# Idle products on TensorE at stage borders and in the mixers' fronts, and tiles turned by ordinary products

## The reference

```
# first block
z = rmsnorm(x) @ w_in ;  u, v, q, k, vv, gate, mq = split(z)
a = gelu(u) * (tril(w_s) @ rmsnorm(gelu(v)) + b_s)              # gMLP, 6 groups
b = softmax(q k^T/8 + cumsum(log_sigmoid(gate)) bias, causal) vv  # 6 heads
c = softmax(mq km^T/8) vm   with km, vm = rmsnorm(mem) @ w_mem_kv # 4 heads, 256 memory rows
x = x + rmsnorm([a, b, c] @ w_out)                              # M1
x = x + rmsnorm(relu(rmsnorm(x) @ w_ff1)^2 @ w_ff2)             # F0, width 4096
# second block, twice:  swiglu(h) = (silu(h @ wg) * (h @ wu)) @ wd, width 2816
x = x + swiglu(rmsnorm(x)) / 2                                  # F1, F3
x = x + sliding_window_attention(rmsnorm(x))                    # MA: 16 heads, 2 kv heads, window 128, sinks, T5 bias
x = x + latent_attention(rmsnorm(x))                            # MB: c = h @ w_in; q = norm(c_q) @ w_uq; k, v = norm(c_kv) @ w_ukv;
                                                                #     16 heads of 64 + 32 rotary, causal
x = x + swiglu(rmsnorm(x)) / 2                                  # F2, F4
```

## Time and profile before

| | us |
|---|---|
| runs | 1295.24, 1296.60, 1297.97 |
| median | 1296.6 |
| profiled execution | 1299.77 |
| its span | 1298.0 |
| PE busy | 1236.5 |
| DVE busy | 886.6 |
| ACT busy | 611.1 |
| POOL busy | 158.7 |

### The profile page before, as it was taken

How to read it: one execution, slowest core, us unless ns; L and a number is a source line. 1 busy time by engine, 2 the same in 40 slices (tenths; PEclk the granted TensorE clock), 3 DMA queues, 4 the chain that set the end, 5 groups by cost and what they waited for, 6 DMA issues and landing times.

```text
span 1298.0 us, 17912 instructions
## 1 busy us (share of the span) xinstructions
PE 1236.5 (95%) x7062; PEld 1065.0 (82%) x7062; DVE 886.6 (68%) x1078; ACT 611.1 (47%) x786; POOL 158.7 (12%) x164
## 2 busy tenths in 40 slices
PE   7998899999899999979999999999999869999998
PEld 7995799999788888866888888888888757888887
DVE  4886565565676776675866776866776475866675
ACT  5556534344443444576543444444344485544342
POOL 2431212012210000240100000100001340100000
PEclk9998899999999999999999999999999889999999
DMA  9773268695685556452555565655553313555530
GB/s 295 223 214 98 67 168 207 163 246 165 172 283 181 191 194 193 145 167 77 190 183 181 191 194 162 201 190 182 182 179 121 122 33 99 194 184 182 185 129 33
DMA packets 165401, 219.62 MB, mean 169 GB/s; under 512 B 13676, under 2 KB 143792, under 8 KB 165212
## 3 DMA queue, kind: packets, MB, share of 16 engines
q1 hardware_dynamic: 155356, 212.28, 51.8%
q0 software_dynamic: 9984, 6.49, 2.9%
HBM read 213.26 MB, written 5.25 MB: 168 GB/s over the span
## 4 chain that ended last, share of the span: by engine, by line
PE 85%; DVE 8%; ACT 4%; issue 1%; POOL 1%; DMA 0%; SPq 0%; DVEq 0%; ACTq 0%
PE ps L276 26%; PE ps L251 14%; PE ps L253 14%; PE ps L252 14%; PE ps L278 13%; DVE w_lo L232 2%; PE ps L555 1%; POOL scratch L799 1%; ACT w_hi L225 1%; PE ps L580 1%; PE ps L568 1%; ACT h_both L436 1%; DVE h_both L444 1%; DVE arena L658 1%; DVE scratch L806 0%
## 5 line engine op out<-in xcount | busy, mean ns | idle before, releaser
L225 ACT CAST w_hi<-raw 128x2048 fp32r<-128x2048 f32 x197 | 374.1, 1899 | 431.5 <-PE ps L278 274.3
L232 DVE TENSOR_TENSOR w_lo<-raw,w_hi 128x2048 fp32r<-128x2048 f32 x194 | 443.1, 2285 | 170.5 <-ACT w_hi L225 169.7
L276 PE MATMUL ps<-h_both,w_hi 128*128 128x512 f32 x1408 | 500.0, 399 | 4.6 <-DVE h_both L444 4.6
L278 PE MATMUL ps<-h_both,w_lo 128*128 128x256 f32 x1408 | 395.2, 281 | 0.0
L276 PEld LDWEIGHTS ps<-h_both,w_hi 128*128 128x128 f32 x1408 | 265.2, 188 | 70.6 <-issue 5.5
L278 PEld LDWEIGHTS ps<-h_both,w_lo 128*128 128x128 f32 x1408 | 266.5, 189 | 1.4
L251 PE MATMUL ps<-w_hi,act_hi 128*128 128x512 f32 x480 | 188.3, 392 | 1.4 <-DVE act_lo L1047 1.4
L253 PE MATMUL ps<-w_hi,act_lo 128*128 128x512 f32 x480 | 187.4, 390 | 0.0
L252 PE MATMUL ps<-w_lo,act_hi 128*128 128x512 f32 x480 | 187.2, 390 | 0.0
L283 DVE TENSOR_REDUCE arena<-ps 128x512 f32<-128x1024 f32 x88 | 107.8, 1225 | 82.4 <-PE ps L278 82.1
L251 PE MATMUL ps<-w_hi,h_both 128*128 128x256 f32 (+3 forms) x324 | 110.6, 341 | 10.2 <-DVE h_both L444 5.0
(11 more groups left out here) (237 smaller groups left out, 1300.9 us busy)
## 6 DMA issues: line engine op xcount, KB each, us to landing
raw<-in_ffn_wg SPq DMA_DIRECT2D x44, 1024.0 KB, 5.4
raw<-in_ffn_wu SPq DMA_DIRECT2D x44, 1024.0 KB, 5.4
raw<-in_ffn_wd SPq DMA_DIRECT2D x44, 1024.0 KB, 4.9
raw<-in_w_ff SPq DMA_DIRECT2D x32, 1024.0 KB, 17.2
raw<-in_w_in SPq DMA_DIRECT2D x8, 1024.0 KB, 11.8
raw<-in_a_w_in SPq DMA_DIRECT2D x5, 1024.0 KB, 5.4
raw<-in_w_out SPq DMA_DIRECT2D x4, 1024.0 KB, 5.1
raw<-in_a_w_out SPq DMA_DIRECT2D x4, 1024.0 KB, 5.0
```

Source lines behind the costliest of these rows:

```text
L225: nc.scalar.copy(w_hi[:, b % RING, 0:n], raw[:, b % RAW, 0:n]).then_inc(hi_ready, 1)
L232: nc.vector.tensor_tensor(w_lo[:, b % RING, 0:n], raw[:, b % RAW, 0:n], w_hi[:, b % RING, 0:n].bitcast(F32), ALU.subtract).then_inc(lo_rea ...
L276: nc.tensor.matmul(ps[:, bank + f, :], hi[:, k, f * P:(f + 1) * P], h_both[:, k, :, :].rearrange("p a b -> p (a b)"), start=k == 0, stop=F ...
L278: last = nc.tensor.matmul(ps[:, bank + f, 0:TOK], lo[:, k, f * P:(f + 1) * P], h_both[:, k, 0, :], start=False, stop=k == KD - 1, skip_gro ...
```

## The change

Three edits. **Turned tiles:** `turned()` issues `nc.tensor.matmul(to, source, ident)` where `nc.tensor.transpose(to, source, ident)` stood, at L391, L568, L967, L968, L1890, L1913, L1987 and L2040; 344 tiles in all. The transposes of the norms' gains (L1862) and of the gMLP's biases (L1891) stay. **Idle products:** `keep_busy(bank, n)` issues n products of `ident` with 256 columns of `tri` into a PSUM bank that nothing reads then. **Places:** 4 before the gains' landing, 5 behind the turn of mem, 5 behind the second projection, 4 before M1's wait for v, in M1's attention 4, 2, 2 ahead of rounds 2, 3, 4; at the border to F0 5 ahead of the turns, 2 amid them and 2 behind, to F1 2, 3, 2, at the other five 0, 0, 3; in MA's attention 1 and 3 ahead of rounds 2 and 3; in MB 6 and 3 behind the latent turns, 6 before q and k are first turned, and 6, 2, 3, 3 ahead of rounds 0 to 3. They are 90 together.

```diff
+        def turned(to, source):
+            return nc.tensor.matmul(to, source, ident[:, :], start=True, stop=True, skip_group_check=True)
+        def keep_busy(bank, count):
+            for _ in range(count):
+                nc.tensor.matmul(ps[:, bank, 0:TOK], ident[:, :], tri[:, 0:TOK], start=True, stop=True, skip_group_check=True)
         def product(to, still, moving, start, stop):
...
+        TURN_IDLE = {2: (5, 2, 2), 3: (2, 3, 2)}
         def plain_tensor_turn(n):
+            ahead, amid, behind = TURN_IDLE.get(n, (0, 0, 3))
+            left = y_bank(n - 2, 0) + 1
+            keep_busy(turn_bank(n) + 3, ahead)
             for t in range(TT):
+                if t:
+                    nc.tensor.wait_ge(x_ready, x_halves(n - 2, 0, 1))
+                    keep_busy(left, amid)
                 for half in range(2):
                         col = (k % 2) * TOK + t * P
-                        last = nc.tensor.transpose(ps[:, turn_bank(n) + k // 2, col:col + P], x[:, t, k * P:(k + 1) * P], ident[:, :])
+                        last = turned(ps[:, turn_bank(n) + k // 2, col:col + P], x[:, t, k * P:(k + 1) * P])
                         if t == TT - 1 and k % 2:
                             last.then_inc(h_psum, 1)
+            keep_busy(left, behind)
...
                         col = s * TOK + t * P - (s * P if h.causal else 0)
-                        last = nc.tensor.transpose(ps[:, 2 + h.e % 2, col:col + P], h.weights(t)[:, s * P:(s + 1) * P], ident[:, :])
+                        last = turned(ps[:, 2 + h.e % 2, col:col + P], h.weights(t)[:, s * P:(s + 1) * P])
                 last.then_inc(turned_psum, 1)
...
-        def attention_tensor(heads, between=None, after=None, begun=0):
+        def attention_tensor(heads, between=None, after=None, begun=0, idle={}, idle_bank=5):
             pairs = pairs_of(heads)
             for n in range(len(pairs) + 3):
+                keep_busy(idle_bank, idle.get(n, 0))
                 if begun <= n < len(pairs):
...
             for t in range(TT):
-                nc.tensor.transpose(ps[0:QK, 6 + h % 2, t * P:(t + 1) * P], qb[:, t, h * QK:(h + 1) * QK], ident[:, :])
-                last = nc.tensor.transpose(ps[0:QK, 6 + h % 2, TOK + t * P:TOK + (t + 1) * P], kc[:, t, h, :], ident[:, :])
+                turned(ps[0:QK, 6 + h % 2, t * P:(t + 1) * P], qb[:, t, h * QK:(h + 1) * QK])
+                last = turned(ps[0:QK, 6 + h % 2, TOK + t * P:TOK + (t + 1) * P], kc[:, t, h, :])
             last.then_inc(qk_psum, 1)
...
             tensor.wait_ge(tables_ready, 1)
+            keep_busy(6, 4)
             tensor.wait_ge(gain_landed, 16 * len(gain_sources))
             norm_tensor_turn(0, mem)
+            keep_busy(6, 5)
...
             project(1)
+            keep_busy(7, 5)
             for p in range(2, 11):
...
             for g in range(G):
-                nc.tensor.transpose(ps[:, 7 - g // 4 * 2, g % 4 * P:(g % 4 + 1) * P], ws[:, g, :], ident[:, :])
+                turned(ps[:, 7 - g // 4 * 2, g % 4 * P:(g % 4 + 1) * P], ws[:, g, :])
             nc.tensor.transpose(ps[:, 5, 256:262], bs, ident[0:6, 0:6]).then_inc(ws_psum, 1)
...
                 if n == 0:
+                    keep_busy(6, 4)
                     tensor.wait_ge(v_ready, 1)
...
                         for t in range(TT):
-                            last = nc.tensor.transpose(ps[:, 6 + k // 2, k % 2 * TOK + t * P:k % 2 * TOK + (t + 1) * P],
-                                                       oa[:, t, k * P:(k + 1) * P], ident[:, :])
+                            last = turned(ps[:, 6 + k // 2, k % 2 * TOK + t * P:k % 2 * TOK + (t + 1) * P],
+                                                       oa[:, t, k * P:(k + 1) * P])
                     last.then_inc(oa_psum, 1)
...
-            attention_tensor(heads_m1, gated_turn, early_rows_m1)
+            attention_tensor(heads_m1, gated_turn, early_rows_m1, idle={2: 4, 3: 2, 4: 2})
             out_m1(6, 1)
...
                             source = qa[:, t, 256 * (p - 1) + c:256 * (p - 1) + c + P] if p else kd[:, t, c:c + P]
-                            last = nc.tensor.transpose(ps[:, A_TURN_BANK[p], k * TOK + t * P:k * TOK + (t + 1) * P], source, ident[:, :])
+                            last = turned(ps[:, A_TURN_BANK[p], k * TOK + t * P:k * TOK + (t + 1) * P], source)
                     last.then_inc(a_turned, 1)
...
-                attention_tensor(heads_a, late_turns, early_rows_a, begun=1)
+                attention_tensor(heads_a, late_turns, early_rows_a, begun=1, idle={2: 1, 3: 3})
                 late_rows("a_out")
...
                             col = (k - chunks[0]) * TOK + t * P
-                            last = nc.tensor.transpose(ps[:, bank, col:col + P], cn[:, t, k * P:(k + 1) * P], ident[:, :])
+                            last = turned(ps[:, bank, col:col + P], cn[:, t, k * P:(k + 1) * P])
                     last.then_inc(c_turned, 1)
+                    keep_busy(*((6, 6), (1, 3))[n - 1])
                     tensor.wait_ge(c_lo, n)
...
                 tokens_out(up + 2, lambda t, c, w: ps[:, t, 0:w])
+                keep_busy(7, 6)
                 tensor.wait_ge(q_squares, 4)
...
-                attention_tensor(heads_b, next_pair, early_rows_b)
+                attention_tensor(heads_b, next_pair, early_rows_b, idle={0: 6, 1: 2, 2: 3, 3: 3}, idle_bank=4)
                 late_rows("b_out")
```

## The result

The changed kernel takes 1320.7 us (median of 4, from 1314.6 to 1326.2) against 1297.0: the ratio is 1.018, 95% interval 1.015 to 1.021. Slower, as forecast, but by 24 us instead of 11, and outside the range of 1297 to 1316.

A forecast was written before the change was run, and what follows sets the result against it. TensorE was taken as the bound, busy 1236.5 of 1298.0 us. Stage terms, clock gains against costs of turns and idle products, summed to +10.85, added to the median 1296.6 for 1307.5; range 1297 to 1316.

The forecast's parts named there:

- F1 border: Border to F1: 1.7 us to gain from the cold stretch, less about 1.1 of delay, -0.6.
- the price of a turn: Each of 344 turned tiles costs TensorE 0.11 us more, 38 us in all, some hidden by waits.
- the loop: Latent mixer's attention: eleven turns lengthen each 4.42 us round by 1.22, +4.9 over four rounds; scores 5.64 apart.
- 4.8 - 3.2: Warm borders: turns and idle products in TensorE's queue decide the first product, +1.6, taken as +1.45 each.
- Start and M1: Start -1.3 us; first mixer's front 0, from -2 to +1.5; its 18 turns where TensorE is full +2.0.
- MB's front: Latent mixer's front: products 4.8 us faster, next cold stretch -1.5, border +1.45, turns of c +0.7; sum -4.15.
- rival B: Clock still falls at F0 and the latent front, idle products delaying there: +20, 1317 us; chance 0.13.
- MA's front: Window mixer's front: half of the turns chained with ScalarE lie on the path, +1.1 us.
- adding the sum to the median: Whole kernel: profiled 1299.8 us called within scatter (3.2 from the median), so the sum was added to 1296.6.
- A: Clock gains at the start of F0 and both big fronts exceed turn costs: -11.5, 1285 us; milder 1294; chance 0.12.
- C: Latent loop absorbs turns, +7.8 becoming +4, and borders cost +1.1 each: +5.6, 1302 us; chance 0.20.
- D: A wash: absorbed turns plus 3 us more gain in the fronts, +2 to +3, about 1299 us; chance 0.10.

The follow-up runs named there:

- again: Second profile of the unchanged changed kernel, from its faster group of executions: 1316.1 us.
- the first profile: Profile of the changed kernel from its slower group of executions: 1325.2 us.
- fill variants: Changed kernel with canvas fills moved: two of four to F1, 1316.3 us; first into M1, 1323.2; start held back until F0's sixth block is split, 1313.5.
- late fills: Kernel before, with the start of its four canvas fills held back until F0's sixth weight block is split: 1297.7 us, ratio 0.9993.
- the lean version: Transposes kept; against idle products alone, those at the five warm borders, in M1, MA and before MB's rounds 1 to 3 removed: 1289.1 us, ratio 0.9945.
- the early fill: First of four canvas fills issued in M1: in the changed kernel 1323.2 us, ratio 1.02; in the lean version 1296.9, ratio 0.9996.

## Why the prediction was wrong

The step that failed is the F1 border, "-0.6", with ScalarE's wait there put at nothing: it measured +10.0 in the executions that stalled. Two of the four executions had the stall, and without it the time was 1315.6, just inside the range. The rest of the miss, +18.6 for +10.85, is three terms of the sum that were too small, and the step from the profiled execution to the median.

Lags by stage, forecast against the profile of "again", both against the profiled execution of before:

| step | forecast | measured |
|---|---|---|
| start, M1 front and its 18 turns | +0.7 | +4.0 |
| F0 border | -2.3 | -2.3 |
| F1 border | -0.6 | -0.65, or +10.0 when stalled |
| MA border | +1.45 | +1.49 |
| MA front and attention | +3.6 | +4.6 |
| F2, F3 borders | +2.9 | +2.8 |
| MB border and front | -4.15 | -2.5 |
| MB attention | +7.8 | +7.5 |
| F4 border | +1.45 | +1.4 |
| sum | +10.85 | +16.3 |

**Right: the price of a turn and where it is paid.** Borders to 0.05 us, the loop at 5.64, 18 turns at the end of M1 +2.1, F0's gain. The step "4.8 - 3.2" (turns and idle products decide, not the rounding) is what the rows show. The warm borders had no clock to win: idle products alone left them as they were.

**Mis-sized, +5.5 in all.** *Start and M1*: in the first profile the start's 1.7 came, but a new cold stretch at 77.5 took 1.5 of it back. In "again" the start was cold at 16.4 to 19.8 and had won 0.1 by 26, and the stretch at 77.9 cost 1.5 besides. M1's own front gave nothing. The lag at 148 is 2.4, 4.0, 1.9 and 1.3 in four profiles of this kernel and its fill variants, so part of it is scatter. Nor was the start's gain one of the idle products: it came without them too, in the turns alone and in the kernel before with late fills. *MB's front*: the products from 999 to 1015 won 4.9 (4.8 forecast). But I took gains up to 1045 that a chain through VectorE and GpSimd ends, and the clock fell there once more, under the idle products that I had counted as hidden: 2 us at the first scores. That is the small form of rival B. *MA's front*: the turns stand on the path nearly whole, not half: +2.2 for +1.1.

**The step that failed by method: adding the sum to the median.** The sum was made against the profiled execution, 1299.8, and added to 1296.6, as if its distance lay within the scatter; but 1299.8 lies outside the runs named there, 1295.24 to 1297.97. It is 2.8 above the median of 1297.0. The changed kernel's profile of the lower group was 0.5 above its own (1316.1, 1315.6). The sum lacked the difference, 2.3 us: 10.85 + 5.5 + 2.3 = 18.6, the lower group. The late fill's trace shows where such 2.3 us can lie: F0's and F1's cold stretches, which it had shorter or not at all. It should have been held open as a term with both signs. (The seven stretches of the earlier trace rows add up to 44.1, not 43.9; nothing hangs on it.)

**Missing altogether, and what carried the time out of the range: the stall.** No rival spoke of transfers. Two of the four executions had it, and the median of four (1320.7) lies between the groups, 5 us above the lower. That it was two of four, when it was six of 16 in all, is chance. The profile of before showed what was needed: weight blocks of F0 landed after 17 us instead of 5, and ScalarE waited 4.2 for the very block. I had put that at nothing without naming how little slack it had.

**The rivals.** A (clock pays more) fell: the idle products alone gained 10, not 25. Without the turns they give 1287.6, the better change. B came in part, C did not (the loop lengthened in full), D did not.

## What to carry to other kernels

Judge a change of two halves by its halves: idle products alone won 10 us, turns by products lost 17.5, and the two overlapped in what they won. Idle work on a waiting engine is free only while it ends before the wait it fills; count it in the engine's own queue together with what else the change put there. And look at every in-order wait near the edge of its slack before trusting a sum of microseconds: here one of 4 to 6 us cost nothing and one of 12 cost 10. And read a gain from more than one trace of the kernel before: of the four cold stretches that looked worth having here, only MB's and part of F0's were there to be won in the second trace.

## What the runs showed of the hardware

- A 128x128 float32 tile costs TensorE 0.11 us as a transpose and 0.22 as a product, and two transposes in place of one product held the clock just as well.
- Where the clock falls is not fixed by TensorE's own instructions there: the lean version held MB's front (lag 4.7 less behind it), and with the early fill, with the same code there, it was at 0.50 from 1006.3 to 1016.5; the start was warm without any idle product in the kernel before with late fills (1.8 us earlier at 31.7).
- One `TENSOR_SCALAR` of VectorE on 128x256 float32 in SBUF stood until GpSimd had issued its transfer (6.75 us): 5.29 us for 0.35, and 4.54 in the lean version with the early fill. VectorE's masks from PSUM (0.28 to 0.42) ran at their usual speed beside the same issue, and `TENSOR_TENSOR` on 128x2048 took its usual 2.29 at 309.51 beside the issue at 307.72 in the kernel before. Nothing else that VectorE started beside a fill's issue, in any of the traces, took clearly longer than elsewhere.
